# RG-LRU, NSA, MoBA and S5 seams of a two-block f32 kernel: queues reordered, first output tiles by other routes

## The reference, cut to what matters

```python
# first block
h = h + (rec * gelu(yb)) @ w_out            # RG-LRU mixer, width 1536
h = h + swiglu(rmsnorm(h, g), w_gu, w_down)
h = h + (g0 * o_cmp + g1 * o_sel + g2 * o_win) @ w_o   # NSA: 16 heads, 3 branches
h = h + swiglu(rmsnorm(h, g), w_gu, w_down)
h = rmsnorm(h, final_g)
# second block, each layer: half ffn, mixer, half ffn (width 2816)
h = h + 0.5 * swiglu_2(...)                 # layer 0: this is the joint FFN below
h = h + (g * sigmoid(g @ w_glu)) @ w_out    # S5 mixer, g = gelu(y)
h = h + 0.5 * swiglu_2(...)
h = h + 0.5 * swiglu_2(...)                 # layer 1
h = h + softmax(q k^T) v @ w_out            # MoBA: 8 heads
h = h + 0.5 * swiglu_2(...)
```

## Time and profile before

| | us |
|---|---|
| median of 3 runs | 1743.94 (1742.52 to 1744.46) |
| profiled execution | 1750.02 |
| its span | 1748.2 |
| TensorE busy | 1709.4 (98%) |
| VectorE busy | 1273.3 (73%) |
| ScalarE busy | 838.3 (48%) |
| GpSimd busy | 377.2 (22%) |
| mean granted TensorE clock | 0.99 |

### The profile page before, as it was taken

The page is one execution under the profiler, slowest core; times in us unless marked ns, Lnnn a source line. Parts: engine busy times, 40 slices in busy tenths (PEclk is TensorE's granted clock), DMA queues, the critical chain, the costliest instruction groups (busy, mean ns, idle before and its releaser), DMA issues.

```text
span 1748.2 us, 31974 instructions
## 1 busy us (share of the span) xinstructions
PE 1709.4 (98%) x12958; PEld 1603.4 (92%) x12958; DVE 1273.3 (73%) x1667; ACT 838.3 (48%) x1110; POOL 377.2 (22%) x425
## 2 busy tenths in 40 slices
PE   7989999999999999999999999999999999999999
PEld 7779999898779999899989989998999989989998
DVE  7898889785858988888766867666666665676663
ACT  5865444443555444454444245444444444554442
POOL 0223012535405123510032121002100127330000
PEclk9999999999899999999999999999999999999999
DMA  8236568675205778555646334554455545335561
GB/s 322 97 117 214 197 216 274 226 271 194 69 1 178 257 243 292 190 182 180 228 157 242 136 139 175 192 206 178 158 181 203 205 153 176 117 130 193 193 226 37
DMA packets 50712, 321.03 MB, mean 184 GB/s; under 512 B 7696, under 2 KB 8912, under 8 KB 20144
## 3 DMA queue, kind: packets, MB, share of 16 engines
q1 hardware_dynamic: 36432, 280.61, 45.4%
q0 software_dynamic: 12736, 36.87, 6.5%
q10 hardware_dynamic: 1440, 2.10, 0.3%
HBM read 307.39 MB, written 10.09 MB: 182 GB/s over the span
## 4 chain that ended last, share of the span: by engine, by line
PE 89%; DVE 7%; ACT 2%; issue 1%; DMA 1%; POOL 0%; ACTq 0%; DVEq 0%
PE bank L2276 18%; PE bank L2270 17%; PE bank L2271 17%; PE bank L2272 17%; PE bank L2277 9%; DVE w_lo L1445 2%; PE bank L2529 1%; PE bank L2712 1%; PE bank L2880 1%; PE bank L2832 1%; PE bank L2601 1%; PE bank L2539 1%; PE bank L2450 1%; DMA vc_other<-vc_raw 1%; ACT w_hi L1019 1%
## 5 line engine op out<-in xcount | busy, mean ns | idle before, releaser
L1445 DVE TENSOR_TENSOR w_lo<-raw,w_hi 128x1024 fp32r<-128x1024 f32 (+2 forms) x492 | 650.0, 1324 | 273.9 <-ACT w_hi L1019 272.5
L1019 ACT ACTIVATE w_hi<-raw 128x1024 fp32r<-128x1024 f32 (+2 forms) x492 | 544.1, 1113 | 605.7 <-PE bank L2272 351.0
L2270 PE MATMUL bank<-hg_hi,w_hi 128*128 128x256 f32 x2648 | 754.4, 285 | 14.1 <-DVE hg_lo L1450 10.4
L2271 PE MATMUL bank<-hg_lo,w_hi 128*128 128x256 f32 x2648 | 750.3, 283 | 0.0
L2272 PE MATMUL bank<-hg_hi,w_lo 128*128 128x256 f32 x2648 | 750.2, 283 | 0.0
L2270 PEld LDWEIGHTS bank<-hg_hi,w_hi 128*128 128x128 f32 x2648 | 509.0, 192 | 19.0 <-DVE w_lo L1445 13.7
L2271 PEld LDWEIGHTS bank<-hg_lo,w_hi 128*128 128x128 f32 x2648 | 509.2, 192 | 0.2
L2272 PEld LDWEIGHTS bank<-hg_hi,w_lo 128*128 128x128 f32 x2648 | 509.2, 192 | 0.0
L2276 PE MATMUL bank<-hid,w_hi 128*128 128x512 f32 x1056 | 372.9, 397 | 0.0
L2277 PE MATMUL bank<-hid,w_lo 128*128 128x256 f32 x1056 | 296.3, 281 | 0.0
L2276 PEld LDWEIGHTS bank<-hid,w_hi 128*128 128x128 f32 x1056 | 198.5, 188 | 48.2 <-issue 1.0
(11 more groups left out here) (407 smaller groups left out, 1930.3 us busy)
## 6 DMA issues: line engine op xcount, KB each, us to landing
raw<-in_w SPq DMA_DIRECT2D x189, 1024.0 KB, 4.9
raw<-in_w SPq DMA_DIRECT2D x48, 1408.0 KB, 6.2
raw<-in_w SPq DMA_DIRECT2D x8, 768.0 KB, 4.2
b_rows<-in_s_b_rows POOLq DMA_DIRECT2D x8, 512.0 KB, 7.7
l_rows<-s_powers POOLq DMA_DIRECT2D x64, 64.0 KB, 9.3
s_ca<-cp_s POOLq DMA_DIRECT2D x8, 512.0 KB, 5.1
s_ba<-ba_s POOLq DMA_DIRECT2D x8, 512.0 KB, 7.8
ba_slot<-s_ba POOLq DMA_DIRECT2D x8, 512.0 KB, 5.4
```

Of the source, the lines that this page charges most:

```text
L1019: act.activation(w_hi[s][:, 0:n], raw[r][:, c * n:(c + 1) * n], ACT.Copy).then_inc(hi_made, 1)
L1445: dve.tensor_tensor(w_lo[s][:, 0:n], raw[r][:, c * n:(c + 1) * n], w_hi[s][:, 0:n].bitcast(F32), ALU.subtract).then_inc(lo_made, 1)
L2270: pe.matmul(psum, w_hi_ap, x_hi_ap, start=first, stop=False, **kw)
L2271: pe.matmul(psum, w_hi_ap, x_lo_ap, start=False, stop=False, **kw)
```

## The change

1. **Plain halves.** Of RG-LRU's output weights the four halves of tiles 0 and 1, of S5's the two halves of tiles 0 and 1, are no longer split (`PLAIN`). TensorE multiplies them in plain f32 straight from `raw` by f32 activations (`rec_f`, now in place in `y_gelu`; `u_s` in S5). `n_split` counts the splits that remain. SyncE reloads those `raw` buffers once TensorE has used them. The tile then has one half in its bank, and `add_to_h` is one instruction.
2. **RG-LRU's queues** on VectorE and ScalarE are reordered around the last scan.
3. **NSA's head.** GpSimd issues one compression piece, not three, ahead of the joins; `turn_queries(6, 3)` comes one half earlier.
4. **NSA's attention start.** Scaling of job 1's exponentials (`factor(1)`) stands right behind `keep_queries(5)`, the compression branch one step later, the last two weight splits in step 5 instead of 2.
5. **Early output products** (`Outward`). In NSA and MoBA, part of output tiles 0 and 1 is made between the last turns, in banks 0 and 1, which the attention no longer needs; k-tiles whose heads are done come first.
6. **Joint FFN.** `close_block` runs in two parts of four tiles, behind the hidden product of pairs 0 and 9.
7. **S5.** Splits of the two plain halves are gone, and only `split(14, 15)` is left beside them.

The diff, cut:

```diff
+        first = 2 * phases[0]["u0"] + 2 * RT
+        PLAIN = list(range(first, first + SPLIT)) if phases[0]["kind"] == "rglru" else []
+        PLAIN += [2 * ph["u0"] + 16 + m for ph in phases if ph["kind"] == "s5" for m in range(2)]
+        def n_split(half):
+            return half + 1 - sum(p <= half for p in PLAIN)
...
         def rec_f(g):
-            slot = GT * (g % 2)
-            return xb[:, slot:slot + GT, 0:T]
+            return y_gelu[:, GT * g:GT * g + GT, :]
...
-                    sp.wait_ge(lo_made, 2 * (unit - RAW) + 2 + 2 * row_step * it)
+                    if 2 * (unit - RAW) in PLAIN:
+                        sp.wait_ge(half_used, 2 * (unit - RAW) + 2)
+                    else:
+                        sp.wait_ge(lo_made, n_split(2 * (unit - RAW) + 1) + 2 * row_step * it)
...
-                for i in range(3):
-                    load_compression(i)
+                load_compression(0)
                 pool.wait_ge(proj_read, base + 2)
...
-                for i in range(3, 6):
+                for i in range(1, 6):
                     load_compression(i)
...
-                for j in range(2 * RT):
+                for j in range(2 * RT - SPLIT):
                     split_hi(half0 + j + SPLIT)
...
+                for u in range(4):
+                    gelu_of_y(u)
+                hi_of_rec(0)
+                gelu_of_y(4)
+                split_hi(half0 + 2 * RT + SPLIT)
+                split_hi(half0 + 2 * RT + SPLIT + 1)
+                hi_of_rec(1)
                 gelu_of_y(5)
                 hi_of_rec(2)
                 hi_of_rec(3)
...
-                attention(att, {7: lambda: compressed_exps(1)},
-                          {1: last_weights, 2: lambda: compressed_probs(0), 3: last_rows, 10: lambda: compressed_probs(1)})
+                attention(att, {2: lambda: compressed_probs(0), 7: lambda: compressed_exps(1)},
+                          {1: last_weights, 2: lambda: compressed_exps(0), 3: last_rows, 10: lambda: compressed_probs(1)})
...
-            def add_to_h(ph, m, psum):
+            def add_to_h(ph, m, psum, parts=2):
+                if parts == 1:
+                    dve.scalar_tensor_tensor(h[:, m, :], psum[:, 0:T], ph["scale"], h[:, m, :], ALU.mult, ALU.add).then_inc(h_written, 1)
+                    return
...
-                        if ph["joint"]:
-                            close_block()
...
                     dve.tensor_tensor(hid_f[:, :], up_s[:, :], silu_s[:, :], ALU.mult).then_inc(hidf_made, 1)
+                    if ph["joint"] and p in (0, 9):
+                        close_block(range(4) if p == 0 else range(4, KT))
...
-                attention(Attention("nsa"), {1: last_queries, 2: last_weights,
+                attention(Attention("nsa"), {1: lambda: keep_queries(5), 2: lambda: compressed_probs(0), 5: last_weights,
                                              4: lambda: masked_scores(1), 6: lambda: compressed_maxima(1), 8: lambda: compressed_probs(1)},
-                          {1: lambda: masked_scores(0)})
-                project(ph, half0 + 28, 1)
+                          {1: lambda: masked_scores(0), 2: lambda: compressed_maxima(0)}, (1,))
+                project(ph, half0 + 28, 1, ATT_BANKS)
...
+                    def plain(m, g, used=0):
+                        for k in range(GT * g, GT * g + GT):
+                            half = half0 + 2 * m + k // 6
+                            r, at = half // 2 % RAW, half % 2 * half_size(half) + k % 6 * P
+                            pe.wait_ge(recf_made, g + 1)
+                            pe.wait_ge(raw_loaded[r], 16 * (half // (2 * RAW) + 1))
+                            last = pe.matmul(bank[REC_BANKS[m]][:, 0:T], raw[r][:, at:at + P], rec_f(g)[:, k % GT, :],
+                                             start=k == 0, stop=k == RT - 1)
+                        if used:
+                            last.then_inc(half_used, used)
...
+                    for g, used in enumerate(((0, 0), (1, 0), (0, 0), (2, 1))):
+                        plain(0, g, used[0])
+                        plain(1, g, used[1])
...
+            class Outward:
...
+                def part(self, m, ks):
+                    hi, lo = weights(self.half0 + m)
+                    for k in ks:
+                        if m == 0:
+                            pe.wait_ge(o_made, self.jobs + 2 * (k // self.per_group) + 2)
+                        last = wide_passes(bank[ATT_BANKS[m]], hi[:, k * P:(k + 1) * P], lo[:, k * P:(k + 1) * P],
+                                           self.x[:, :, k, :], k == 0, k == KT - 1)
...
                     turn(n)
+                    if n in behind_turns:
+                        behind_turns[n]()
...
+                def first_tiles():
+                    outward.part(0, range(4, 6))
+                    outward.part(1, range(2))
...
+                          {14: lambda: outward.part(0, range(4)), 15: first_tiles})
+                outward.part(1, range(2, 6))
+                outward.part(0, range(6, 8))
+                outward.part(1, range(6, 8))
+                outward.rest()
...
+                          {3: lambda: outward.part(0, range(4))})
...
+                for mp in range(4):
+                    pe.wait_ge(gated, mp + 1)
+                    for m in range(2):
+                        for k in (2 * mp, 2 * mp + 1):
+                            at = m * HALF["w8"] + k * P
+                            last = pe.matmul(bank[2 + m][:, 0:T], raw[r][:, at:at + P], u_s[:, k, :], start=k == 0, stop=k == KT - 1)
```

More of the change, by code:

```diff
@@ L674, in _ @@
                     run = min(run, RAW)
-                if run >= 2 * BODY:
+                if run >= 2 * BODY and not any(2 * (unit + i) in PLAIN for i in range(run)):
                     trips = run // BODY
@@ L1462, in joint_gains, with close_block @@
                 dve.wait_ge(joint_made, 1)
-            def close_block():
-                dve.wait_ge(jrms_made, 1)
-                own(dve.reciprocal(joint_rstd[:, :], joint_rstd[:, :]))
-                for m in range(KT):
+            def close_block(tiles):
+                if tiles.start == 0:
+                    dve.wait_ge(jrms_made, 1)
+                    own(dve.reciprocal(joint_rstd[:, :], joint_rstd[:, :]))
+                for m in tiles:
                     dve.scalar_tensor_tensor(h[:, m, :], h[:, m, :], gain("final", m), joint_rstd[:, :],
@@ L1491, in project @@
                     half = half0 + m * per_tile
-                    if per_tile == 2:
+                    plain = half in PLAIN
+                    if per_tile == 2 and (m or not plain):
                         split_lo(half + SPLIT)
                     dve.wait_ge(half_used, half + per_tile)
-                    add_to_h(ph, m, bank[banks[m % 2]])
-                    split_lo(half + per_tile - 1 + SPLIT)
+                    add_to_h(ph, m, bank[banks[m % len(banks)]], 1 if plain else 2)
+                    if m or per_tile == 1 or not plain:
+                        split_lo(half + per_tile - 1 + SPLIT)
                     if ph["next"]:
@@ L1849, in attention @@
                         behind_maxima[n]()
-                    if n >= 1:
+                    if n >= 1 and n - 1 not in done:
                         factor(n - 1)
@@ L1853, in attention @@
                         at_step[n]()
+                    if n in done:
+                        factor(n)
                     if n - 1 >= (split_jobs + 2) * att.branches:
@@ L2331, in two_from_hg, with project @@
                     tile(c, KT - 1).then_inc(half_used, 1)
-            def project(ph, half0, halves, per_half, x, ready):
-                for m in range(KT):
+            def project(ph, half0, halves, per_half, x, ready, first=0):
+                for m in range(first, KT):
                     if m >= 2:
@@ L2514, in token_major, with __init__, rest, attention @@
                 last.then_inc(half_used, 1)
-            def attention(att, score, pv, step_waits, after_scores, at_step):
+            class Outward:
+                def __init__(self, ph, half0, x, per_group, jobs):
+                    self.ph, self.half0, self.x, self.per_group, self.jobs = ph, half0, x, per_group, jobs
+                def part(self, m, ks):
[5 more added lines that the diff above has]
+                                           self.x[:, :, k, :], k == 0, k == KT - 1)
+                    if k == KT - 1:
+                        last.then_inc(half_used, 1)
+                def rest(self):
+                    for m in range(2, KT):
+                        if m >= 4:
+                            pe.wait_ge(h_written, h_count(self.ph["hw"], m - 2))
+                        self.part(m, range(KT))
+            def attention(att, score, pv, step_waits, after_scores, at_step, behind_turns):
                 def scores(n):
@@ L2732, in rows_and_kept @@
                 def rows_and_kept():
+                    compressed_probs(0)
```

(6 more changed lines are left out.)

84 lines of the change are left out of this document (33 added, 51 removed).

## The result

The changed kernel takes 1725.86 us (median of 4 runs, 1725.17 to 1726.57), the kernel before 1743.23 in the same comparison (1741.03 to 1744.46): a ratio of 0.990, 95% interval 0.9885 to 0.9919. That is 17.4 us less. The forecast was 1717, 26.9 less than the median of before that it started from; the time lies inside the range of 1710 to 1729.

A forecast was written before the change was run, and what follows sets the result against it. The prediction took TensorE's gaps and the slow clock behind them as the bound; seven gains sum to 28.0 us, 1743.94 - 28.0 = 1715.9, and one expected wait of about 1 us makes 1717, eight-in-ten range 1710 to 1729.

The forecast's parts named there:

- What bounds the kernel: Whole kernel: TensorE bounds it, busy 1709.4 of 1748.2 us; gaps, together 39 us, and slow clock behind several can be shortened.
- RG-LRU: RG-LRU's end: plain products and reordered queues remove TensorE's wait before tile 2; gain 6.4 us, bounds 0 and 8.5.
- Joint FFN: Joint FFN: four of eight scalings moved behind the hidden product remove TensorE's 2.77 us wait; gain 2.8, bounds 1.2 and 2.9.
- MoBA: MoBA's end: four early output products fill the 1.18 us gap before the last value products; gain 1.2, bounds 0 and 1.2.
- the start of NSA's attention: NSA's first steps: two gaps and slow clock, 8.3 us, less 2.0 new waits and 0.8 for splits; taken as 5.0.
- the second rival: VectorE is the bound: RG-LRU, both NSA terms and S5 each lose 2 to 4 us; about 1729, chance 0.13.
- the head: NSA's head: fewer compression pieces ahead of the joins remove a 1.78 us gap and 1.4 of slow clock; gain 3.2.
- NSA's end: Last two turns of NSA: early output products fill gaps of 1.27 and 1.18 and save 2.75 slow clock; gain 5.2.
- S5: S5's end: two tiles as plain products take 7.1 us instead of 11.29; gain 4.2, bounds 1 and 5.6.
- The sum 28.0: Whole kernel: all seven gains added, giving 1722.0 on the profiled execution and 1715.9 on the median.
- The first rival: New short waits keep the slow clock at NSA's start and most of its end; gain 21, about 1723, chance 0.2.
- The slow side: NSA attention from 468 to 510: clock stays down, 39 us more, about 1755, slower than before; chance 0.03.

The follow-up runs named there:

- close_one: Changed kernel with all eight scalings of the joint FFN's residual ahead of the gate product, as before: median 1728.53 us, 2.7 more.
- lo_step10: Changed kernel with VectorE's last two weight splits of NSA in step 10 instead of step 5: median 1719.51 us, 6.3 less.
- the second profile of before: The kernel before, without any edit, profiled once more: 1740.62 us, with a span of 1738.8.
- pool_order: Changed kernel with GpSimd's old order at NSA's head, three compression pieces ahead of the joins: median 1727.99 us, 2.1 more.
- nsa_late: Changed kernel with all output products of NSA behind its attention: median 1728.15 us, 2.3 more.
- s5_split: Changed kernel with S5's first two output tiles split again: median 1728.92 us, 3.1 more.
- moba_late: Changed kernel with MoBA's output products all behind its attention: three comparable runs of 1724.19, 1724.36 and 1727.14 us, 1.5 less by their median.

## Why the forecast was 9 us too low

The time lies in the range, but the total hides one term that came to nothing and a base that did not fit. *What bounds the kernel* was right: each gain is a gap of TensorE or slow clock behind one. *RG-LRU* (6.4): 6.9 against either profile. A part of that is slow clock from 113 to 119, which the prediction did not name; both profiles of before have it. *Joint FFN* (2.8): 3.0 against the first profile, 4.2 against the second, which has the slow clock behind the gap, and 2.7 by close_one. *MoBA* (1.2): 1.0.

**The step that failed is the start of NSA's attention**, taken as +5.0. Between the first and the last scores the changed kernel loses 1.5 us against the profile that I read and 4.1 against the other one; with the 1.7 us gap ahead of the first scores, which did go, the term is +0.2 and -2.4. The first part of the working held: in the changed kernel's trace step 2's turn is over at 447.81, 6.2 us better than in before's (465.36) when both are taken from the last query product ahead of the first scores (429.60 and 440.93); 8.3 less the two waits of 2.0 is 6.3. The 0.8 us that I charged for the two splits in step 5 were wrong: they cost a 3.27 us gap and the slow clock behind it, 6.3 us by the median of lo_step10. I had read that VectorE is busy for 14.22 of 16 us there, and then charged by its idle share instead of following its queue to the scaling that TensorE waits for; and I had priced the splits without looking at what GpSimd does beside them. It was in the rows: VectorE as the bound in step 5 was part of the second rival.

**The second error is in the base.** Four terms were read as start to end in one execution, with the slow clock in them: 1.4 at the head, 4.8 at the start, 2.75 at the end of NSA, and about 2.7 in S5. In the second profile of before those clocks are 1.00, 0.87, 1.00 and 1.00. So the head (3.2) is 3.6 against the first profile, 0.9 against the second and 2.1 by pool_order; NSA's end (5.2) is 5.2, 2.3, and 2.3 by nsa_late; S5 (4.2) is 4.4, 1.7, and 3.1 by s5_split. The sum 28.0 was made for the profiled execution, where 24.85 came, and then subtracted from the median, which has less of the slow clock to give. With 2.1, 2.3 and 3.1 for these three and -2.4 for the start the sum is 6.9 + 2.1 - 2.4 + 2.3 + 2.8 + 3.1 + 1.0 = 15.8. It mixes differences of medians and of profiles, so that it comes near the 17.4 measured is a rough check only; the second profile, from which the -2.4 is taken, lies 2.6 below before's median itself. The time stayed in the range because the range was wide, not because the sum was good: 9 of the 12 us that it left above the forecast are used up, 5 to 7 by the start of the attention and the rest by the base.

The first rival was half right: slow clock did stay, behind the new gap. The slow side did not come: behind each gap the clock was back within 13 us, in every profile.

## What to carry to other kernels

Follow the queue of the helper engine, instruction by instruction, to the one that the bound engine waits for; a busy share of 89% says nothing on which of them is late. Put background work into a step in which the helper idles (in the changed kernel VectorE waits 2.97 us for TensorE in step 10) and GpSimd does not work beside it. A slow clock behind a gap of 1 to 3 us is no fixed cost: price it from two profiles, or set the gap alone as the lower end and gap plus clock as the upper.

## What the hardware showed that I had not expected

- Behind gaps equal to 0.02 us the clock fell in one execution and not in the other: two gaps of 1.27 and 1.17 us at NSA's end have a mean clock of 0.66 behind them in one profile and 1.00 in the other. The same holds between kernels with one and the same code at this place: behind a gap at the start of NSA's attention the 6 us from 443.5 have a clock of 0.50 in moba_late (gap of 1.23) and 1.00 in close_one (1.22). The kernel before scatters over 1739.3 to 1748.5 us in one comparison, the version with no fall in the attention over 1718.9 to 1720.2. The gap of the changed kernel in step 5 (3.24 to 3.28 us) had the slow clock behind it in all five profiles that show it. The Trainium skill, "TensorE: Matmul & The Clock Gate", section "What's actually happening", has that activity is judged in windows that run free of the kernel. By that rule it is a matter of where a gap lands; no run here varies that by itself.
- VectorE's splits of 128x1024 take 1.2 us alone and 2.3 beside GpSimd's products of 24x512, and GpSimd's 2.13 instead of 1.26. That GpSimd works on 24 partitions only makes it no cheaper for VectorE.
- A plain f32 product of 128x128x256 takes 0.42 us in a row of 24 (0.424) and of 16 (0.421), less than the 0.4425 of the eight in before, against 0.353 for the split one, whose parts two other engines have to make first.
